# Starting TensorE's loop over pairs of experts at the first instruction of a fetch block

## The reference, cut to what matters

```python
def moe_swiglu(h, router_w, w_gu, w_down):
    probs = jax.nn.softmax((h @ router_w).astype(jnp.float32), axis=-1)
    top_p, top_i = lax.top_k(probs, TOP_K)
    top_p = top_p / jnp.sum(top_p, axis=-1, keepdims=True)
    gates = jnp.sum(jax.nn.one_hot(top_i, N_EXPERTS, dtype=jnp.float32) * top_p[..., None],
                    axis=-2).astype(h.dtype)
    y = jnp.zeros_like(h)
    for e in range(N_EXPERTS):
        y = y + gates[..., e:e + 1] * swiglu(h, w_gu[e], w_down[e])
    return y
```

## Time and profile before

| what | value |
|---|---|
| median of 3 runs | 2000.62 us (1999.05 to 2005.67) |
| time of the profiled execution | 2002.98 us |
| its span, first to last instruction | 2001.5 us |
| TensorE busy in the span | 1904.1 us, 95% |
| mean granted TensorE clock | 0.985 |
| packets of the queue that brings TensorE's instructions (q8) | 175, 2.87 MB |

### The profile page before, as it was taken

How to read it: one execution, slowest core, us unless ns; L and a number is a source line. 1 busy time by engine, 2 the same in 40 slices (tenths; PEclk the granted TensorE clock), 3 DMA queues, 4 the chain that set the end, 5 groups by cost and what they waited for, 6 DMA issues and landing times. The chain is left out here.

```text
span 2001.5 us, 39754 instructions
## 1 busy us (share of the span) xinstructions
PE 1904.1 (95%) x14657; PEld 1550.6 (77%) x14658; DVE 1121.7 (56%) x1761; ACT 754.9 (38%) x1299; POOL 431.8 (22%) x360
## 2 busy tenths in 40 slices
PE   7899999999999999999999998999999999999994
PEld 5788888888886478787888776788887787787872
DVE  4676777677675654223222367665558558554337
ACT  4533442442341022221222213655547447453332
POOL 0245334435422222121121244100000000000003
PEclk9899999999999999999999998999999999999998
DMA  8233234224335352243323615976569669664344
GB/s 277 97 120 123 71 117 141 83 91 149 96 97 179 107 175 98 84 138 116 100 82 95 233 55 180 338 262 213 181 219 336 208 213 340 220 211 148 111 148 173
DMA packets 185077, 321.57 MB, mean 161 GB/s; under 512 B 26143, under 2 KB 77239, under 8 KB 184839
## 3 DMA queue, kind: packets, MB, share of 16 engines
q1 hardware_dynamic: 170567, 287.05, 43.6%
q0 software_dynamic: 8144, 28.84, 3.9%
q10 hardware_dynamic: 6128, 2.30, 0.4%
HBM read 285.45 MB, written 32.67 MB: 159 GB/s over the span
## 5 line engine op out<-in xcount | busy, mean ns | idle before, releaser
L1381 PE MATMUL pp<-whi,xTh 128*128 128x512 f32 (+1 forms) x1152 | 442.6, 384 | 17.0 <-issue 11.5
L1383 PE MATMUL pp<-wlo,xTh 128*128 128x512 f32 (+1 forms) x1152 | 431.3, 374 | 0.0
L1382 PE MATMUL pp<-whi,xTl 128*128 128x512 f32 (+1 forms) x1152 | 431.0, 374 | 0.0
L2121 ACT ACTIVATE whi<-raw_halves 128x1024 fp32r<-128x1024 f32 (+1 forms) x256 | 245.3, 978 | 113.9 <-PE pp L1383 100.7
L1381 PEld LDWEIGHTS pp<-whi,xTh 128*128 128x128 f32 x1152 | 218.1, 189 | 57.8 <-issue 16.8
L1383 PEld LDWEIGHTS pp<-wlo,xTh 128*128 128x128 f32 x1152 | 218.1, 189 | 38.7
L1382 PEld LDWEIGHTS pp<-whi,xTl 128*128 128x128 f32 x1152 | 218.6, 190 | 35.0
L2775 DVE TENSOR_TENSOR wlo<-raw_halves,whi 128x1024 fp32r<-128x1024 f32 (+1 forms) x144 | 167.6, 1164 | 109.0 <-ACT whi L2121 82.4
L1381 PE MATMUL pp<-whi,hTh 128*128 128x512 f32 x503 | 202.4, 402 | 4.5 <-DVE ybuf L2727 2.3
L2784 DVE TENSOR_TENSOR wlo<-raw_halves,whi 128x1024 fp32r<-128x1024 f32 (+1 forms) x144 | 159.2, 1106 | 77.8 <-ACT whi L2121 64.0
L1383 PE MATMUL pp<-wlo,hTh 128*128 128x512 f32 x503 | 196.6, 391 | 0.0
(11 more groups left out here) (354 smaller groups left out, 3289.3 us busy)
## 6 DMA issues: line engine op xcount, KB each, us to landing
raw_halves<-in_moe_w_gu SPq DMA_DIRECT2D x320, 256.0 KB, 4.3
wring<-in_ada_w SPq DMA_DIRECT2D x80, 512.0 KB, 4.7
raw_halves<-in_moe_w_down SPq DMA_DIRECT2D x160, 256.0 KB, 3.5
wring<-in_ffn_w_gu SPq DMA_DIRECT2D x80, 256.0 KB, 2.9
wring<-in_dn_w_in SPq DMA_DIRECT2D x124, 128.0 KB, 2.8
wring<-in_ffn_w_down SPq DMA_DIRECT2D x40, 256.0 KB, 3.0
expert_in<-zeros SPq DMA_DIRECT2D x36, 256.0 KB, 3.3
wring<-in_ada_first SPq DMA_DIRECT2D x32, 256.0 KB, 6.3
```

Source lines behind the costliest of these rows:

```text
L1381: pe.matmul(out, hi[:, c0 + c, tt], wh, start=(first and c == 0), stop=False)
L1382: pe.matmul(out, lo[:, c0 + c, tt], wh, start=False, stop=False)
L1383: mm = pe.matmul(out, hi[:, c0 + c, tt], wl, start=False, stop=(last and c == nk - 1))
L2121: act.activation(whi[:, hs, 0:nk, 0:w], raw_half(l, k, s)[:, 0:nk, 0:w], ACT.Copy)\
```

## The change

```diff
--- before.py
+++ after.py
@@ -1483,7 +1483,7 @@
 
                 if l:
                     rn, rc = expert_counts(pe, n0)
-                    with nc.Fori(0, 4, engines=[pe.engine], hint_back_edge=True) as pair:
+                    with nc.Fori(0, 4, engines=[pe.engine], hint_back_edge=True, head_slot={pe.engine: 0}) as pair:
                         for i in range(2):
                             n, c = this_expert(pe, rn, rc)
                             n2 = expert(2 * pair + i, n, c)
```

## The result

The changed kernel took 2008.79 us, the median of 21 runs (2003.97 to 2013.29), beside 2003.20 us for the kernel before in 21 runs (1998.50 to 2007.27). The ratio is 1.0027, with a 95% interval of 1.0020 to 1.0035: it is slower by some 5.5 us. The profiled execution took 2008.40 us, its span is 2006.9 us.

What follows compares the result with a forecast made beforehand. TensorE was taken to bound the kernel, busy 1904.1 of 2001.5 us. Median 2000.6 plus 5.0 (4.3 lost at three closing branches, 0.7 clock) gave 2005.6 us, range 1999 to 2012.

Steps and rivals of the forecast that it cites:

- The fetch, one block ahead: In the loop, each block is asked for when the one before is entered; ready 5.8 (pass 1) or 6.65 us later.
- The padding: Ahead of the loop: one taken branch, once, before a matmul that waits for VectorE anyway; 0 us added.
- The first block of a pass: Behind the closing branch: the block is now full, jumps of 3.00 and 2.08 us become short; gain 0.
- Pass 0: At its closing branch the head is asked for at 1403.0 instead of 1399.3 us: 1.2 us lost, 0 to 2.4.
- Pass 1: At its end the last block comes a little late, then the head takes 5.5 us: 2.0 us lost, 0 to 4.3.
- Pass 2: At its end the head is asked for at 1702.9 us and takes 6.2 us: 1.1 us lost, 0 to 2.9.
- rival B: In one-tile experts, last two blocks both late, two waits in a row, clock low longer: 12 us, 2013; chance 0.15.
- The clock: Behind the gaps at pass ends, a longer gap may add to the low granted clock: 0.7 us, range 0 to 4.
- Inside the loop: Block boundaries inside experts: 21 blocks per pass remain, so 0 us, with 2 us either way.

Runs made afterwards that it cites:

- slot 137: Changed kernel with head_slot 137 instead of 0, where the loop lay in the kernel before: 2003.35 us, ratio 1.0006 to the kernel before.
- slots 237 and 238: Changed kernel with head_slot 237 or 238 instead of 0: 2004.89 us, ratio 1.0008, and 2018.78 us, ratio 1.0078, to the kernel before.
- slot 180: Changed kernel with head_slot 180 instead of 0: 1999.77 us, ratio 0.9984 to the kernel before.
- two further kernels: Kernel before with its loop written out as eight experts, the first starting at slot 150 or 180: 1996.91 us (0.9963) and 1995.10 us (0.9953).

## Why the prediction was right, point by point

The forecast was 2005.6 us from a base of 2000.6, plus 5.0. The measured difference is 5.6 us by the medians, 5.4 by the ratio. That 2008.8 stands 3 us above the forecast is mostly the base, which came out 2.6 us higher over 21 runs than over 3.

- **The fetch, one block ahead.** Right, and shown: in pass 0 the lead goes with the slot (without the hint the closing branch waits 3.5 us more at slot 137, 1.0 at slot 0), and at slots 237 and 238 the wait moves from the closing branch to the next block and to both. Single jumps of 3.56 and 3.69 us between consecutive blocks leave no room for a fetch that runs several blocks ahead.
- **The padding.** Right: nothing, by the 1.50 us for VectorE that the first matmul of the loop waits with and without it. Slot 137, meant as the test, has no padding.
- **The first block of a pass.** Right: the jumps of 3.00 and 2.08 us behind the closing branch are gone (233 ns is the longest in 8 us behind it), and it gained nothing.
- **Pass 0.** Predicted a closing branch of 3.5 to 4.5 us and 1.2 us lost; it took 4.30 and lost 1.51. The fetch took 4.5 us from the entry of the last block (1403.79 to 1408.26), where I had 4.0.
- **Pass 1.** Predicted 2.0 lost, measured 2.65. The total was nearly right, its parts less so: the jump into the last block took 2.9 us, where I had it about 0.7 late, since that block's fetch took 7.1 us (1549.28 to 1556.37) and not 5.4; the head then took 4.5, where I had 5.5. That the two errors nearly cancel is luck.
- **Pass 2.** Predicted 1.1 lost, measured 1.21, in the same two parts (2.2 and 5.2 us). My sum had only the second: it let the head be asked for at 1702.9 us, without the wait for the last block that pass 1 was given. The head's fetch made up for it in part, with 5.4 us for my 6.2. So this number is luck too, and rival B's two waits in a row did occur; its price didn't, since the first of them was over at 1707.66 us and TensorE ran dry only at 1707.94.
- **The clock.** 0.7 taken, 0.9 measured.
- **Inside the loop.** 0 taken, with 2 either way; measured -0.8 in one execution. It isn't quiet, though: +1.4 and -1.6 us in two experts with the same number of tiles.

That sum, 5.4 + 0.9 - 0.8, is 5.5 us, while the loop of this one execution is 3.8 longer. Most of what is missing, 1.0 us, is in pass 1; it may be in gaps too short to stand as waits, and was not settled. It is within the 2 us by which the loop differs between two executions of the same list (693.3 and 691.3 us). So the mechanism and the size of the whole are borne out, and that 5.0 lies within 0.6 us of the measured difference is closer than its parts warrant. The rest of the 5.4 us of span is the later start of the loop, which varies by some us from execution to execution whatever the slot.

## What to carry to other kernels

For a loop whose blocks are all fetched anew in each pass (84 packets for four passes of 21 blocks here), count the body modulo the block (256 instructions here): what mattered at the back edge here was how much *time*, not how many instructions, lay between the entry of the last block and the closing branch, and between the head and the next boundary. A body of a whole number of blocks and a few instructions, started at slot 0, puts those few into a block of their own: of the five slots tried in the loop only 238 was slower (1.0078 against 1.0027). Code that is jumped over gave hardly any lead (0.3 us for 43 instructions at slot 180). If the list may grow, write the loop out (0.9962 here); if not, keep both end blocks well filled (0.9984 at slot 180), keep the hint (without it 0.0031 more at slot 0 and 0.0029 at slot 137), and look at the durations of the branches themselves, which show a wait that no busy engine shows (up to 5.17 us in the changed kernel, where a jump inside a block took 0.22).

## What the runs showed of the hardware that was not expected

- A taken closing branch left 0.48 to 0.52 us before the first matmul behind it started, where TensorE had run dry (1555.36 to 1555.84, 1408.26 to 1408.78).
- At slot 0 without a hint two instruction packets fell into the 5 us of the closing branch of pass 0; with it there was one.
- The granted clock was 0.54 over the 10 us behind a gap of 5.24 us, 0.77 behind 5.56, 0.83 behind 2.91, and 1.00 behind 2.50 at slot 180: the length of the gap alone didn't tell what the clock did.
- An experiment at one fixed place can mislead: one profiled execution at slot 180 suggested a rule for the boundaries inside experts which two further kernels did not bear out.
